# VectorE instead of GpSimd for the unit sums and three low parts in the FFN passes of a hybrid decoder step

## The chip, the cores and the metric

One Trainium2 chip, one core of it. The metric is the device time in microseconds (us) of one execution of the whole kernel. Engine names as in the profile: PE is TensorE, DVE is VectorE, ACT is ScalarE, POOL is GpSimd, SP is SyncE, which issues most DMAs.

## The reference, cut to what matters

One layer on 1024 prompt tokens and 8 sample tokens (1032 columns here), model width 1024, FFN width 2816, all in float32:

```
h = x + 0.5 * swiglu(rmsnorm(x, ffn1_norm), w_gate, w_up, w_down)
p = rmsnorm(h, mix_norm) @ w_in
h = h + concat(s5_mixer(...), short_conv(...)) @ w_out
h = h + 0.5 * swiglu(rmsnorm(h, ffn2_norm), w_gate, w_up, w_down)
y = rmsnorm(h, final_norm)
swiglu(x, wg, wu, wd) = (silu(x @ wg) * (x @ wu)) @ wd
```

The change touches only the two FFNs.

## The kernel before, in words

Activations lie transposed in SBUF, channels on partitions, the 1032 columns in three blocks of 344. Every float32 product is made of three matmuls: an operand is split into a high part (rounded to fp32r, a copy by ACT) and a low part (raw minus high, a subtraction), and PE computes high*high, high*low and low*high (`product3`, L1128 to L1130).

Both FFNs run mostly in "passes" (`ffn_passes`). A pair of passes p takes two columns of 128 of the FFN width: the even pass t computes their gate part, the odd pass t+1 their up part. The weights of a pass are four quarters of 128x512, called A11, A12, A21, A22; a Strassen-Winograd scheme needs four sums of them too: S1 = A21 + A22, S2 = S1 - A11, S3 = A11 - A21, S4 = A12 - S2. Each of the eight is a "unit" with a slot: raw `UR`, high `UH`, low `UL`. UL lies on the memory of UR, so a raw unit that is still to be read must be read before its low part is made. A21 and A22 are loaded into two staging tiles `AST`; the others into their slot.

A pass has eleven products in the order V1a, V1b, M1, M2, M6, M5, M7, V2a, M3, M4, V2b, each of four chunks, each chunk of three matmuls; chunks are numbered 0 to 43. In an even pass PE puts one step of the down projection of the pair before behind each chunk from number 7 on (36 steps, of which eight, named P1 and P2, are twice as long). DVE adds each step's bank to HT (`step_add`, L2549), which frees the bank: five banks go round, and the step that next uses a bank waits for that addition (`pair_free`).

Work around it in a pass: ACT makes the eight high parts of the next pass in an order written out by hand, copies M1, M6 and M7 out of PSUM ("copied"; M6 waits for the copy of M1, M7 for that of M6, in the same bank), and does silu. DVE makes low parts (`unit_lo` of DVE, L2510), combines sums c11, c22, c12 (L2585; V2a, M3 and the pass after next wait for them), multiplies gate and up (L2600, L2606), mixes and splits the hidden tiles for the down projection (`mix_h` L2570, `h_lo2` L2611) and the down weights (`mix_quarter` L2523 to L2528, `quarter_lows` L2532 and L2515). DVE's order is by chunk number in even passes and by product name in odd ones. POOL makes S1 to S4 of a pass (`make`, L3188 to L3198), each after the last product of the pass before that used the slot, then the low parts of A21, A22 and S4 (L3206). PE waits for each low part by `unit_ready`.

SP issues the loads in one order. The load of A21 or A22 into AST waits until the low part of the pass before is made from that tile, and until S3 or S1 of that pass is made (L936 to L941); the loads of A11 and of down weights stand behind it in the queue.

Passes 2 to 17 are in FFN 1 and 20 to 39 in FFN 2: 36 passes, 18 pairs. The first two passes of each FFN are plain (no sums); before the first pass with sums DVE has an order of its own at the top level (`mul_plain`, `x_unit_lo`, L2623, and others).

Of the kernel before, what the change touches and what calls it, by code (L numbers as in the profile page):

```python
# [332 lines left out]
def loads_count(t, unit):  # L333

    e, n = stage(t)
    return e * (PASSES[0] - 1) + max(n, 1) if unit in (A11, A12) else e * PASSES[0] + n + 1
# [23 lines left out]
def hybrid_trunk(nc, a, o):  # L360
# [11 lines left out]
    with ctx:  # L372
# [1897 lines left out]
        def _(dve):  # L2270
# [229 lines left out]
            def unit_lo(t, k):  # L2500
                if stage(t)[1] >= 2 and k == A11:
                    dve.wait_ge(s_made, made_count(t, S3))
                if stage(t)[1] >= 2 and k in (A12, S2):
                    dve.wait_ge(s_made, made_count(t, S4))
                if k == S1:
                    dve.wait_ge(s_made, made_count(t, S2))
                slot = slot_of(t, k)
                raw = AST[k - 2] if k in (A21, A22) else UR[slot]
                dve.wait_ge(u_hi, hi_count(t, k))
                dve.tensor_tensor(UL[slot][:, :], raw[:, :], f(UH[slot][:, :]), ALU.subtract).then_inc(unit_ready[slot], 1)  # L2510
# [24 lines left out]
            def quarter_lows(n):  # L2535
                if n // 4 not in LAST_PAIR:
                    sums_lo(n)
                quarter_lo(n)
# [51 lines left out]
            def c22(t):  # L2590
                combine(t, "M5", "M7", "v", (1, 2))
# [29 lines left out]
            def x_unit_lo(e, u):  # L2621
                dve.wait_ge(xu_hi, (len(XU_ORDER) + XN) * e + XU_ORDER.index(u) + 1)
                dve.tensor_tensor(xl(e, u), t_raw(e, u), f(xh(e, u)), ALU.subtract).then_inc(xu_ready[u], 1)  # L2623

            def t_step(out, x, y, op, waits=None):
                if waits is not None:
                    dve.wait_ge(t_made, waits)
                dve.tensor_tensor(out, x, y, op).then_inc(t_made, 1)

            def ffn_passes(e):  # L2630
                for t in range(FIRST[e] + 2, LAST_PASS[e] + 1):
                    p, g = divmod(t, 2)
                    more = t < LAST_PASS[e]
                    if g == 0:
                        for chunk in range(4 * len(ORDER)):
                            for n in range(STEPS):
                                if STEP_AFTER[n] + 1 == chunk:
                                    step_add(p - 1, n)
                            if chunk == 9:
                                h_lo2(p - 1, 7)  # L2640
                            if chunk == 10:
                                h_lo2(p - 1, 8)
                            if chunk == 12 and t == FIRST[e] + 2:
                                quarter_lows(4 * p - 3)
                            if chunk == 11:
                                unit_lo(t, S2)
                            if chunk == 13:
                                unit_lo(t, S1)
                            if chunk == 14:
                                mix_quarter(4 * p - 2)  # L2650
                            if chunk == 16:
                                c11(t)
                            if chunk == 18:
                                quarter_lows(4 * p - 2)
                            if chunk == 20:
                                unit_lo(t, S3)
                            if chunk == 23:
                                mix_quarter(4 * p - 1)
                            if chunk == 26:
                                quarter_lows(4 * p - 1)  # L2660
                            if chunk == 29:
                                c22(t)
                            if chunk == 33:
                                unit_lo(t + 1, A11)
                            if chunk == 32 and p not in LAST_PAIR:
                                mix_quarter(4 * p)
                            if chunk == 35:
                                unit_lo(t + 1, S1)
                            if chunk == 37:
                                c12(t)  # L2670
                            if chunk == 39:
                                unit_lo(t + 1, A12)
                            if chunk == 41 and p in LAST_PAIR:
                                quarter_lo(4 * p)
                                quarter_lo(4 * p + 1)
                    else:
                        dve.wait_ge(pair_full, step_base(p))
                        for name in ORDER:
# [6 lines left out]
                            if name == "M1":  # L2685
                                unit_lo(t, S3)
                                h_lo2(p, 0)
                            if name == "M2":
                                c11(t)
                                mul_sum(t, "C11", (0, 1))  # L2690
                                if p not in LAST_PAIR:
                                    quarter_lows(4 * p)
                            if name == "M6" and p not in LAST_PAIR:
                                quarter_lows(4 * p + 1)
                            if name == "M7":
                                c22(t)
                                mul_sum(t, "C22", (1, 2))
                                if p not in LAST_PAIR:
                                    unit_lo(t + 1, A11)
                            if p not in LAST_PAIR:  # L2700
                                if name == "M3":
                                    c12(t)
                                    mul_sum(t, "C12", (0, 2))
                                    mix_h(p, T3)
                                    mix_h(p, T1)
                                    unit_lo(t + 1, A12)
                                    h_lo2(p, 1)
                                    mix_h(p, T2)
                                    h_lo2(p, 2)
                                if name == "M4":  # L2710
                                    mul(t, "M4", "x", (1, 1))
                                    h_lo2(p, 3)
                                    mix_h(p, T4)
                                    h_lo2(p, 4)
                                    h_lo2(p, 5)
                                if name == "V2b":
                                    mul(t, "V2b", "y", (1, 0))
                                    h_lo2(p, 6)
                                continue
# [65 lines left out]
            mul_plain(0, 3)  # L2785
            mix_h(0, T2)
            mix_h(0, T3)
            unit_lo(2, A11)
            h_lo2(0, 2)
            x_unit_lo(0, T2)  # L2790
            h_lo2(0, 3)
            mix_quarter(1)
            unit_lo(2, A12)
            mul_plain(0, 4)
            mix_h(0, T4)
# [165 lines left out]
            mul_plain(1, 3)  # L2961
            mix_h(PAIR0[1], T2)
            mix_h(PAIR0[1], T3)
            unit_lo(FIRST[1] + 2, A11)
            h_lo2(PAIR0[1], 2)
            x_unit_lo(1, T2)
            h_lo2(PAIR0[1], 3)
            mix_quarter(4 * PAIR0[1] + 1)
            unit_lo(FIRST[1] + 2, A12)
            mul_plain(1, 4)  # L2970
            mix_h(PAIR0[1], T4)
# [44 lines left out]
        def _(pool):  # L3016
# [162 lines left out]
            pool.wait_ge(consts_in, 16 * 5)  # L3179
            pool.nop().then_inc(disc_p, 2)  # L3180

            def make(t, k):

                pool.wait_ge(products, slot_free(t, k))
                if k == S1:
                    pool.wait_ge(a_in[A21], 16 * loads_count(t, A21))
                    pool.wait_ge(a_in[A22], 16 * loads_count(t, A22))
                    ins = pool.tensor_tensor(UR[S1][:, :], AST[0][:, :], AST[1][:, :], ALU.add)  # L3188
                elif k == S2:
                    pool.wait_ge(a_in[A11], 16 * loads_count(t, A11))  # L3190
                    pool.wait_ge(s_made, made_count(t, S1))
                    ins = pool.tensor_tensor(UR[S2][:, :], UR[S1][:, :], UR[A11][:, :], ALU.subtract)
                elif k == S3:
                    ins = pool.tensor_tensor(UR[S3][:, :], UR[A11][:, :], AST[0][:, :], ALU.subtract)
                else:
                    pool.wait_ge(a_in[A12], 16 * loads_count(t, A12))
                    pool.wait_ge(s_made, made_count(t, S2))
                    ins = pool.tensor_tensor(UR[S4][:, :], UR[A12][:, :], UR[S2][:, :], ALU.subtract)  # L3198
                ins.then_inc(s_made, 1)

            def unit_lo(t, k):

                pool.wait_ge(u_hi, hi_count(t, k))
# [2 lines left out]
                pool.tensor_tensor(UL[slot][:, :], raw[:, :], UH[slot][:, :].bitcast(F32), ALU.subtract  # L3206
                                   ).then_inc(unit_ready[slot], 1)

            def ffn_passes(e):
                for t in range(FIRST[e] + 2, LAST_PASS[e] + 1):  # L3210
                    make(t, S1)
                    make(t, S2)
                    make(t, S3)
                    make(t, S4)
                    unit_lo(t, A21)
                    unit_lo(t, A22)
                    unit_lo(t, S4)

            ffn_passes(0)
            norm(1)  # L3220

            tab = UNITS[("tab", 2)]
# [66 lines left out]
            for k in PLAIN_HI:  # L3289
                unit_lo(FIRST[1], k)  # L3290
            norm(2)
            ffn_passes(1)

            pool.wait_ge(gf_in, 16)
            for i, n in enumerate(BY_SCALAR):
# [23 lines left out]
```

## Time and profile before

| | |
|---|---|
| median of 3 runs | 1779.7 us (1779.49 to 1780.2) |
| the profiled execution | 1779.56 us |
| its span, first to last instruction | 1777.7 us |
| busy: PE, DVE, ACT, POOL | 1761.6, 1316.3, 652.3, 644.3 us |
| granted TensorE clock, mean | 0.998 of full |

Busy time is time in which the engine executes an instruction. The span is 1.9 us shorter than the device time of the same execution. PE's matmuls overlap, so that a row shows 320 ns for one while the next starts some 157 ns later.

### The profile page before, as it was taken

What the parts mean: (1) busy time and instruction counts of PE and PEld (TensorE: products, weight loads), DVE (VectorE), ACT (ScalarE), POOL (GpSimd) and SP (SyncE); (2) the same over time, 40 slices, a digit from 0 to 9 for tenths busy, and PEclk for the clock granted to TensorE, in tenths of its full rate; (3) what the DMA queues carried; (4) which work ended last, traced back from release to release, by engine and by line L of the source; (5) the groups of instructions that cost most, each with busy time, mean ns of one, the idle gap of its engine ahead of it and who ended that gap; (6) DMA issues with size and microseconds to landing.
All of it is one profiled execution on the core that took longest, in us unless ns stands there. A gap on an engine that the chain in (4) does not pass through costs nothing.

```text
span 1777.7 us, 31737 instructions
## 1 busy us (share of the span) xinstructions
PE 1761.6 (99%) x11953; PEld 1749.4 (98%) x11953; DVE 1316.3 (74%) x2429; ACT 652.3 (37%) x1281; POOL 644.3 (36%) x669
## 2 busy tenths in 40 slices
PE   8999999999999999999999999999999999999998
PEld 7999999999999999999999999999999999999998
DVE  7658878777877876823775769977887797788766
ACT  7411333333333333533112545333333333333324
POOL 2688232332333232203995221223233332323321
PEclk9999999999999999999999999999999999999999
DMA  6132111111111111355113501111111112111112
GB/s 174 36 131 84 54 54 48 55 48 57 46 54 54 48 54 43 143 128 128 48 42 110 174 14 54 47 56 48 54 48 54 54 43 60 48 54 48 54 49 96
DMA packets 162647, 119.75 MB, mean 67 GB/s; under 512 B 10258, under 2 KB 156242, under 8 KB 161988
## 3 DMA queue, kind: packets, MB, share of 16 engines
q1 hardware_dynamic: 157012, 110.10, 20.9%
q0 software_dynamic: 864, 5.28, 0.9%
q10 hardware_dynamic: 4624, 2.36, 0.6%
q8 instruction: 99, 1.62, 0.4%
q14 instruction: 48, 0.39, 0.1%
HBM read 102.01 MB, written 15.72 MB: 66 GB/s over the span
## 4 chain that ended last, share of the span: by engine, by line
PE 96%; DVE 2%; ACT 1%; issue 0%; DVEq 0%; POOL 0%; POOLq 0%
PE bank_pair L1128 26%; PE bank_pair L1130 25%; PE bank_pair L1129 25%; PE bank_down L1128 6%; PE bank_down L1130 6%; PE bank_down L1129 6%; DVE HT L2298 1%; DVE XL L2321 1%; PE bank_pair L1542 0%; PE bank_pair L1515 0%; PE bank_pair L1638 0%; PE bank_pair L1534 0%; PE bank_pair L1236 0%; PE bank_down L1278 0%; DVE S L2315 0%
## 5 line engine op out<-in xcount | busy, mean ns | idle before, releaser
L1128 PE MATMUL bank_pair<-XHM,U_hi 128*128 128x344 f32 x720 | 230.5, 320 | 0.2 <-DVE XLM L2343 0.2
L1129 PE MATMUL bank_pair<-XLM,U_hi 128*128 128x344 f32 x720 | 229.7, 319 | 0.0
L1130 PE MATMUL bank_pair<-XHM,U_lo 128*128 128x344 f32 x720 | 229.7, 319 | 0.0
L2549 DVE SCALAR_TENSOR_TENSOR HT<-bank_pair,HT 128x344 f32<-128x344 f32 x378 | 186.2, 508 | 51.0 <-PE bank_pair L1130 50.8
L3206 POOL TENSOR_TENSOR U_lo<-AST,U_hi 128x512 fp32r<-128x512 f32 x74 | 106.0, 1435 | 266.1 <-ACT U_hi L1702 266.1
L1128 PE MATMUL bank_pair<-XH,U_hi 128*128 128x344 f32 x608 | 194.1, 319 | 0.0
L1130 PE MATMUL bank_pair<-XH,U_lo 128*128 128x344 f32 x608 | 194.1, 319 | 0.0
L1129 PE MATMUL bank_pair<-XL,U_hi 128*128 128x344 f32 x608 | 194.0, 319 | 0.0
L1128 PE MATMUL bank_pair<-XH,WH 128*128 128x344 f32 x576 | 186.7, 324 | 5.0 <-DVE XL L2321 4.9
L1130 PE MATMUL bank_pair<-XH,WL 128*128 128x344 f32 x576 | 184.2, 320 | 0.0
L1129 PE MATMUL bank_pair<-XL,WH 128*128 128x344 f32 x576 | 184.2, 320 | 0.0
L3188 POOL TENSOR_TENSOR U_raw<-AST 128x512 f32<-128x512 f32 x36 | 48.1, 1336 | 352.3 <-PE bank_pair L1130 314.9
L1702 ACT ACTIVATE U_hi<-U_raw 128x512 fp32r<-128x512 f32 x224 | 138.9, 623 | 93.6 <-DMA U_raw<-in_ffn_w_up 47.9
L2549 DVE SCALAR_TENSOR_TENSOR HT<-bank_down,HT 128x344 f32<-128x344 f32 x270 | 133.9, 506 | 21.5 <-PE bank_down L1130 20.9
L1129 PE MATMUL bank_pair<-XLX,U_hi 128*128 128x344 f32 x448 | 143.4, 320 | 0.0
L1130 PE MATMUL bank_pair<-XHX,U_lo 128*128 128x344 f32 x448 | 143.1, 320 | 0.0
L1128 PE MATMUL bank_pair<-XHX,U_hi 128*128 128x344 f32 x448 | 143.1, 319 | 0.0
L2510 DVE TENSOR_TENSOR U_lo<-U_raw,U_hi 128x512 fp32r<-128x512 f32 x186 | 138.1, 743 | 0.0
L1128 PEld LDWEIGHTS bank_pair<-XHM,U_hi 128*128 128x128 f32 x720 | 135.2, 188 | 0.6 <-DVE XLM L2343 0.5
L1129 PEld LDWEIGHTS bank_pair<-XLM,U_hi 128*128 128x128 f32 x720 | 135.2, 188 | 0.0
L1130 PEld LDWEIGHTS bank_pair<-XHM,U_lo 128*128 128x128 f32 x720 | 135.2, 188 | 0.0
L1927 ACT ACTIVATE HH<-HR 128x344 fp32r<-128x344 f32 x110 | 52.3, 489 | 197.8 <-DVE HR L2600 79.0
(398 smaller groups left out, 4922.7 us busy)
## 6 DMA issues: line engine op xcount, KB each, us to landing
DQ_raw<-in_ffn_w_down SPq DMA_DIRECT2D x52, 256.0 KB, 2.7
U_raw<-in_ffn_w_gate SPq DMA_DIRECT2D x40, 256.0 KB, 3.0
AST<-in_ffn_w_gate SPq DMA_DIRECT2D x40, 256.0 KB, 2.9
U_raw<-in_ffn_w_up SPq DMA_DIRECT2D x40, 256.0 KB, 3.3
AST<-in_ffn_w_up SPq DMA_DIRECT2D x40, 256.0 KB, 2.9
RAW<-in_w_in SPq DMA_DIRECT2D x16, 512.0 KB, 4.0
DQR<-in_ffn_w_down SPq DMA_DIRECT2D x25, 256.0 KB, 2.6
X<-in_x_prompt SPq DMA_DIRECT2D x8, 512.0 KB, 8.6
```

The lines of the kernel that those rows point to most:

```text
L1128: pe.matmul(out, wh, xh, start=first, stop=False, skip_group_check=onto)
L1129: pe.matmul(out, wh, xl, start=False, stop=False, skip_group_check=onto)
L1130: return pe.matmul(out, wl, xh, start=False, stop=last, skip_group_check=onto)
L1702: act.activation(UH[slot][:, :], src[:, :], ACT.Copy).then_inc(u_hi, 1)
L1927: act.activation(h_hi_of(p, form), h_raw_of(p, form), ACT.Copy).then_inc(h_high, 1)
L2298: ins = dve.tensor_tensor(ht, tile, ht, ALU.add)
L2321: dve.tensor_tensor(XL[:, c, cols(tb)], ring(i), f(XH[:, c, cols(tb)]), ALU.subtract).then_inc(xn_low, 1)
L2510: dve.tensor_tensor(UL[slot][:, :], raw[:, :], f(UH[slot][:, :]), ALU.subtract).then_inc(unit_ready[slot], 1)
L2549: dve.scalar_tensor_tensor(ht, STEP_BANKS[STEP_BANK[n]][:, 0:TW], 0.5, ht, ALU.mult, ALU.add).then_inc(pair_free, 1)
L3188: ins = pool.tensor_tensor(UR[S1][:, :], AST[0][:, :], AST[1][:, :], ALU.add)
L3206: pool.tensor_tensor(UL[slot][:, :], raw[:, :], UH[slot][:, :].bitcast(F32), ALU.subtract).then_inc(unit_ready[slot], 1)
```

## The change

`make` goes from POOL's program to DVE's, without a change of its waits, and so do the low parts of A21, A22 and S4 of every pass with sums. POOL's `ffn_passes` goes. In DVE's order the new instructions stand at fixed places, in even passes by chunk, in odd passes by product, and before the first such pass of each FFN among the top level's lines.

```
             def make(t, k):
-                pool.wait_ge(products, slot_free(t, k))
+                dve.wait_ge(products, slot_free(t, k))
...
-            def ffn_passes(e):            # POOL
-                for t in range(FIRST[e] + 2, LAST_PASS[e] + 1):
-                    make(t, S1)
-                    make(t, S2)
-                    make(t, S3)
-                    make(t, S4)
-                    unit_lo(t, A21)
-                    unit_lo(t, A22)
-                    unit_lo(t, S4)
...
# DVE, even pass t
+                            if chunk == 8 and t == FIRST[e] + 2:
+                                unit_lo(t, A21)
+                            if chunk == 12:
+                                unit_lo(t, A22)
+                            if chunk == 21:
+                                unit_lo(t, S4)
+                            if chunk == 25:
+                                make(t + 1, S1)
+                            if chunk == 27:
+                                make(t + 1, S2)
+                            if chunk == 30:
+                                make(t + 1, S3)
+                            if chunk == 38:
+                                make(t + 1, S4)
+                            if chunk == 40:
+                                unit_lo(t + 1, A21)
...
# DVE, odd pass t
                             if name == "M1":
                                 unit_lo(t, S3)
                                 h_lo2(p, 0)
+                                unit_lo(t, A22)
                             if name == "M2":
                                 c11(t)
                                 mul_sum(t, "C11", (0, 1))
+                                unit_lo(t, S4)
...
                             if name == "M7":
+                                if more:
+                                    make(t + 1, S1)
                                 c22(t)
                                 mul_sum(t, "C22", (1, 2))
+                                if more:
+                                    make(t + 1, S2)
+                                    make(t + 1, S3)
                                 if p not in LAST_PAIR:
                                     unit_lo(t + 1, A11)
...
                                 if name == "M3":
                                     c12(t)
                                     mul_sum(t, "C12", (0, 2))
                                     mix_h(p, T3)
                                     mix_h(p, T1)
+                                    make(t + 1, S4)
                                     unit_lo(t + 1, A12)
+                                    unit_lo(t + 1, A21)
                                     h_lo2(p, 1)
...
# DVE, before the first pass with sums of FFN 1 (FFN 2 alike, for FIRST[1] + 2)
             mul_plain(0, 3)
             mix_h(0, T2)
             mix_h(0, T3)
+            for k in (S1, S2, S3):
+                make(2, k)
             unit_lo(2, A11)
...
             mix_quarter(1)
+            make(2, S4)
             unit_lo(2, A12)
```

## Rows read from the trace of the kernel before

**Rows 1.** The page, part 1: busy time, share of the span, instructions.

```profile
PE 1761.6 (99%) x11953; PEld 1749.4 (98%) x11953; DVE 1316.3 (74%) x2429; ACT 652.3 (37%) x1281; POOL 644.3 (36%) x669
```

**Rows 2.** Waits of PE, whole span: us in total, times, longest us.

```profile
PE bank_pair L1128 <- DVE XL L2321: 4.9, 3, 3.2
...
PE bank_pair L1128 <- DVE XLM L2343: 0.2, 1, 0.2
```

**Rows 3.** Windows (us of the stretch; busy, instructions; clock, DMA share, GB/s).

```profile
215.50:697.00 481.50, 481.50 (x3062) 481.50 (x3061) 381.82 (x732) 170.32 (x341) 150.50 (x106) 1.00 0.17 51
1125.00:1717.00 592.00, 592.00 (x3764) 592.00 (x3763) 473.70 (x911) 211.85 (x424) 185.85 (x131) 1.00 0.17 52
...
1241.20:1282.80 41.60, 41.60 (x267) 41.60 (x266) 36.72 (x75) 14.24 (x29) 10.25 (x7) 1.00 0.17 52
1282.80:1303.50 20.70, 20.70 (x133) 20.70 (x133) 12.80 (x23) 8.23 (x17) 9.56 (x7) 1.00 0.18 52
```

**Rows 4.** Unit tiles: count, min/median/max ns, first and last start.

```profile
L2510 DVE TENSOR_TENSOR U_lo<-U_raw,U_hi x186: 672/681/1352, 139.7 to 1724.0; 128x512 fp32r<-128x512 f32 x186
L3206 POOL TENSOR_TENSOR U_lo<-AST,U_hi x74: 1282/1304/1674, 212.6 to 1720.1; 128x512 fp32r<-128x512 f32 x74
L3206 POOL TENSOR_TENSOR U_lo<-U_raw,U_hi x38: 1281/1562/2007, 215.1 to 1721.3; 128x512 fp32r<-128x512 f32 x38
...
L3188 POOL TENSOR_TENSOR U_raw<-AST x36: 1283/1332/2093, 184.5 to 1697.8; 128x512 f32<-128x512 f32 x36
```

**Rows 5.** Timeline of DVE, one pair: start, duration, work, idle before.

```profile
1248.26 1.39 DVE L2611 TENSOR_TENSOR XTL<-XTR,XTH 128x344 fp32r<-128x344 f32 x1
...
1261.69 1.37 DVE L2524 TENSOR_TENSOR SR<-DQ_raw 128x128 f32<-128x128 f32 x1
...
1266.35 1.79 DVE L2515 TENSOR_TENSOR DQ_lo<-DQ_raw,DQH 128x512 fp32r<-128x512 f32 x1
1268.06 1.35 DVE L2549 SCALAR_TENSOR_TENSOR HT<-bank_pair,HT 128x344 f32<-128x344 f32 x3
1269.33 0.50 DVE L2585 TENSOR_TENSOR T<-bank_pair,T 128x344 f32<-128x344 f32 x1
```

**Rows 6.** Timeline of POOL in the same pair.

```profile
1261.58 1.33 POOL L3188 TENSOR_TENSOR U_raw<-AST 128x512 f32<-128x512 f32 x1 [10.78 <-PE bank_pair L1130]
```

**Rows 7.** Timeline of DVE in the odd pass of that pair.

```profile
1287.65 0.52 DVE L2611 TENSOR_TENSOR HL<-HR,HH 128x344 fp32r<-128x344 f32 x1
...
1299.76 0.52 DVE L2585 TENSOR_TENSOR HR<-bank_pair,HR 128x344 f32<-128x344 f32 x1 [0.61 <-PE bank_pair L1130]
...
1301.50 1.49 DVE L2570 TENSOR_TENSOR XTR<-HR 128x344 f32<-128x344 f32 x1
...
1303.94 0.51 DVE L2611 TENSOR_TENSOR HL<-HR,HH 128x344 fp32r<-128x344 f32 x1
```

**Rows 8.** Timeline of ACT in the odd pass.

```profile
1291.84 0.62 ACT L1702 ACTIVATE U_hi<-U_raw 128x512 fp32r<-128x512 f32 x1
1292.36 0.44 ACT L1917 ACTIVATE HR<-bank_pair 128x344 f32<-128x344 f32 x1
```

**Rows 9.** SP's issues in the odd pass; last row: a load's landing time.

```profile
1285.56 0.37 SPq L942 DMA_DIRECT2D AST<-in_ffn_w_gate  x1
1288.45 2.25 SPq L942 DMA_DIRECT2D U_raw<-in_ffn_w_gate  x2
...
U_raw<-in_ffn_w_up SPq DMA_DIRECT2D x1, 256.0 KB, 3.2
```

**Rows 10.** Timeline of DVE before and at the first pass with sums.

```profile
201.48 0.50 DVE L2618 TENSOR_TENSOR T<-bank_pair,T 128x344 f32<-128x344 f32 x1
...
211.17 1.59 DVE L2623 TENSOR_TENSOR XLX<-XRX,XHX 128x1376 fp32r<-128x1376 f32 x1
212.83 0.52 DVE L2549 SCALAR_TENSOR_TENSOR HT<-bank_down,HT 128x344 f32<-128x344 f32 x1
213.76 0.52 DVE L2549 SCALAR_TENSOR_TENSOR HT<-bank_down,HT 128x344 f32<-128x344 f32 x1 [0.42 <-PE bank_down L1130]
```

More of the change, by code:

```diff
@@ L2623, in x_unit_lo, with make @@
                 dve.tensor_tensor(xl(e, u), t_raw(e, u), f(xh(e, u)), ALU.subtract).then_inc(xu_ready[u], 1)
+            def make(t, k):
+                dve.wait_ge(products, slot_free(t, k))
+                if k == S1:
+                    dve.wait_ge(a_in[A21], 16 * loads_count(t, A21))
+                    dve.wait_ge(a_in[A22], 16 * loads_count(t, A22))
+                    ins = dve.tensor_tensor(UR[S1][:, :], AST[0][:, :], AST[1][:, :], ALU.add)
+                elif k == S2:
+                    dve.wait_ge(a_in[A11], 16 * loads_count(t, A11))
+                    dve.wait_ge(s_made, made_count(t, S1))
+                    ins = dve.tensor_tensor(UR[S2][:, :], UR[S1][:, :], UR[A11][:, :], ALU.subtract)
+                elif k == S3:
+                    ins = dve.tensor_tensor(UR[S3][:, :], UR[A11][:, :], AST[0][:, :], ALU.subtract)
+                else:
+                    dve.wait_ge(a_in[A12], 16 * loads_count(t, A12))
+                    dve.wait_ge(s_made, made_count(t, S2))
+                    ins = dve.tensor_tensor(UR[S4][:, :], UR[A12][:, :], UR[S2][:, :], ALU.subtract)
+                ins.then_inc(s_made, 1)
             def t_step(out, x, y, op, waits=None):
@@ L2963, in _ @@
             mix_h(PAIR0[1], T3)
+            for k in (S1, S2, S3):
+                make(FIRST[1] + 2, k)
             unit_lo(FIRST[1] + 2, A11)
@@ L2968, in _ @@
             mix_quarter(4 * PAIR0[1] + 1)
+            make(FIRST[1] + 2, S4)
             unit_lo(FIRST[1] + 2, A12)
@@ L3180, in _ @@
             pool.nop().then_inc(disc_p, 2)
-            def make(t, k):
-                pool.wait_ge(products, slot_free(t, k))
[L3185 to L3199, printed above, removed]
             def unit_lo(t, k):
@@ L3207, in unit_lo @@
                                    ).then_inc(unit_ready[slot], 1)
-            def ffn_passes(e):
-                for t in range(FIRST[e] + 2, LAST_PASS[e] + 1):
-                    make(t, S1)
-                    make(t, S2)
-                    make(t, S3)
-                    make(t, S4)
-                    unit_lo(t, A21)
-                    unit_lo(t, A22)
-                    unit_lo(t, S4)
-            ffn_passes(0)
             norm(1)
@@ L3291, in _ @@
             norm(2)
-            ffn_passes(1)
             pool.wait_ge(gf_in, 16)
```

## The prediction

> **What bounds the kernel now.** I read the page's busy line first: PE is busy for 1761.6 of 1777.7 us, DVE for 1316.3, POOL for 644.3 [rows 1]. Then who PE waited for: in the whole span three waits for the low parts of the first FFN's input (4.9 us) are the largest entry, and the only one from a pass-like stage is 0.2 us at the entry of FFN 2 [rows 2]. Then the stages: from 215.5 to 697 and from 1125 to 1717 us, which is nearly all of the 36 passes, PE is busy for every one of 481.50 and 592.00 us at full granted clock [rows 3]. So in the stretches that the change touches there is nothing to win: every low part and every freed bank already comes in time. The question is only whether it still does when DVE makes them, and how much each was early.
>
> PE's clockwork gives the due times. A pair of passes is 132 groups of three matmuls (88 in the even pass with its down steps, 44 in the odd one) and takes 62.3 us (the last two windows of [rows 3] together), so a group is u = 0.472 us. The sum c12 of the odd pass starts at 1299.76, directly when M3's last group (the 36th) has ended [rows 7]; so that odd pass starts at 1299.73 - 36u = 1282.74 and its even pass at E = 1282.74 - 88u = 1241.20.
>
> **What moves.** Four `make` in each of 36 passes are 144 instructions, and of POOL's 74 + 38 low parts [rows 4] all but the four of FFN 2's first plain pass are 108: together 252, or 14 in a pair. On POOL each takes 1.3 us or more [rows 4]. On DVE a low part of the same shape takes 0.681 us (median) [rows 4]; as neighbouring DVE instructions overlap by some 0.08 us (1268.06 + 1.35 against a next start at 1269.33, [rows 5]) I count 0.60 each. DVE's price for a `make` doesn't stand in the trace: one that reads what the one before wrote can't overlap it, 0.72; 0.60 is the lower end. 14 x 0.60 = 8.4 us more DVE work in a pair, to 10.1 at the upper end.
>
> What DVE gets back: beside POOL's instructions some of DVE's are stretched. SR<-DQ_raw of 128x128, 0.28 us otherwise, took 1.37 at 1261.69, beside POOL's S1 (1261.58 to 1262.91) [rows 5, 6]; between 1241.2 and 1303.5 eight are, the first at 1248.26 (1.39), the last at 1301.50 (1.49, against 0.5) [rows 5, 7], by 7.2 us together. DVE is busy for 36.72 + 12.80 = 49.5 of 62.3 us [rows 3]; afterwards 49.5 + 8.4 - 7.2 = 50.7. Over 18 pairs: + 151 - 130, DVE ends near 1337 us of the span, POOL near 644 - 18 x 19.8 = 287.
>
> The Trainium skill ("SBUF — State Buffer", "SBUF: two separate sides") says that a port pair shared by DVE and GpSimd is an exclusive lock, which a DVE instruction with two SBUF inputs also needs, and that the loser blocks for the whole instruction. The rows agree: only two-SBUF-input instructions are stretched, the PSUM additions (0.50 to 0.52) are not. By that rule all 7.2 us come back; without it none would, which is a rival below.
>
> **Place by place in the steady pair** (before, after; due):
>
> Even pass, the tightest place: M3 waits for c22. M3's first group is number 62 of the pass, 1241.20 + 62u = 1270.46; c22 ended at 1269.33 + 0.50 = 1269.83 [rows 5], 0.63 us early, because DVE had run behind the banks. After: the down step with number n ends at E + (9 + 2n + P)u, P being the long ones so far. Step 15 ends at 1261.0, addition 0.43, mix 0.93: 1262.4. Step 16 is there at 1262.45, 17 at 1263.4; S1 until 1264.4; addition 18, two low parts of down weights until 1266.05; addition 19, S2 until 1267.1; additions 20 and 21 until 1267.95; c22 ends at 1268.45. That is 1.4 us earlier than before although two `make` stand ahead of it, since the mix (1.37 and one more) and the low part at 1266.35 (1.79) lose their stretches [rows 5]. The banks: a step bank must be added within 5u = 2.36 us (6u for M7's); the latest, number 19, is done 1.3 us after its end. From there to the pass's end the queue gets S3, S4 and the low part of A21 in chunks of 0.94 us or more that hold one addition of 0.43 and at most one 0.60: no backlog above 0.6 us. The low part of A22 and of S4 in chunks 12 and 21 come 8 us or more before M4 and M3.
>
> Odd pass, its end: the low parts of hidden tiles for the next pass's down steps. c12 at 1299.76 stays; behind it `mul_sum` and the mix T3 get back 0.6 and 1.0 (1.49 at 1301.50 [rows 7]), S4 and A21's low part cost 1.2 to 1.3. The low part that started at 1303.94 [rows 7] starts at 1303.6 and isn't due before 1303.54 + 8u = 1307.3. A12's low part ends near 1303.1, due at 1305.4.
>
> The waits that DVE now takes on itself: each `make` waits for a product. In the odd pass S1 is put before c22 and waits for M5, which ends at 1282.74 + 24u = 1294.07, while c22 can't start before M7 has ended and been copied, 1296.5. Behind S1 nothing else is queued, so nothing is lost; S2, S3 and S4 stand where their products are over. S1 also waits for A21's and A22's loads, next.
>
> Loads: SP issued A22's at 1285.56 after POOL's low part, and the next A11's at 1288.45 when its product freed it [rows 9]. After: DVE makes A22's low part behind the one at 1287.65 [rows 7], until 1288.77, so A22 is issued at 1288.8 and A11 behind it at 1289.2. Landing takes 3.2 us in such a double issue [rows 9]: 1292.4. S1 at 1294.07 isn't touched. ACT, which took A11's high part at 1291.84 and then copied M6 at 1292.36 [rows 8], does it some 0.6 us later: the copy ends at 1293.4, M7 is due at 1282.74 + 24u = 1294.07. 0.7 us are left. This is the closest place after the change. In the even pass A21's low part ends at 1280.0 instead of 1277.4 and holds up a down-weight load by 3 us: DVE's mix at the odd pass's start waits about 0.5 us, before a stretch in which it idles anyway.
>
> **Entry of each FFN** (no steady state): four `make` stand in the top-level order, and A21's low part behind the first addition. In FFN 1 DVE is free for `mul_plain(0, 3)` at 201.05 (0.4 earlier than 201.48); then four `make` with their dependences (2.9 us), less 0.6 of waits for ACT that they cover: the last x part starts at 213.15 instead of 211.17, and the first addition at 214.65 instead of 212.83 [rows 10]. Its M6 is due at: addition 1 waited for step 1 at 213.73 [rows 10], so the pass began at 208.54 and M6 at + 14u = 215.15; the addition ends at 215.17, the next, behind A21's low part, at 216.2 against 16u = 216.1. About 0.15 us lost; FFN 2's entry comes out alike. Bounds: 0, and with everything 1 us later 2 us for both. I take + 0.2.
>
> Sum: 0 for 18 pairs, + 0.2 for the entries. 1779.56 + 0.2 = 1779.8 for a run like the profiled one; that run lies 0.1 below the median, so 1779.9.
>
> **Rivals.** (a) Slower, DVE becomes the bound in the even pass: if the stretches are DVE's own and stay, c22 ends at 1269.83 + 1.2 = 1271.0, 0.6 after its due time, in each of 18 pairs: + 11, 1790.7. It decides once DVE is 0.63 us later than before at that place. For it: only the coincidence in time speaks against. The skill's "Perfetto Trace Analysis", "Optimizing Scalar/DVE Operations", would hand work of a saturated DVE to GpSimd, but adds that the two may not help each other; DVE isn't saturated here. Chance 0.03.
> (b) Slower, the load chain of the odd pass: A22's low part on DVE later than 0.7 us after my count, or landing over 3.9 us: ACT holds M6's copy, M7 waits. Another 0.5 us beyond that is 16 x 0.5 = 8 us: 1788. The three steps are regular to 0.1 us; 0.05.
> (c) Faster: PE would have to start matmuls closer together or lose waits. In the passes there is one of 0.2 us [rows 2]; 1779.5 at best from that, and over 0.2% nothing gives. 0.01.
> (d) As forecast, 0.91; its own range 1779.3 to 1781.0.
>
> 0.2% is 3.6 us, about what a measurement can tell here. Same 0.92 (the forecast and small forms of b), slower 0.07, faster 0.01. Range 1779.1 to 1782: the runs before spread over 0.7 us, and the upper side takes the entries' bound.
>
> **What would show it.** PE without waits in both long windows; DVE's low parts all near 0.68, busy near 1337; POOL without instructions in the passes, near 287; c22 of the even pass over 1 us before M3; ACT's copy of M6 within 0.7 us of before; a PE wait on HT of some tenths at each entry. Wrong: any PE wait that comes back in every pair, or stretched DVE instructions with POOL silent.

## The result, and the profile after

The changed kernel takes 1785.13 us (median of 6 runs, 1784.98 to 1786.99), the kernel before 1779.87 (6 runs, 1779.42 to 1780.59). The ratio is 1.0031 with an interval of 1.0021 to 1.0041: slower by 5.3 us, 3.7 to 7.3. Forecast were 1779.9, range 1779.1 to 1782.0, with 0.07 on slower. The forecast was wrong. Most of the loss came the way of rival (b), which had 0.05, though as single events and not in every pair; the rest came at the entries and in even passes.

Part 1 of the page, of the kernel after, answers to [rows 1]; below it the page's chain by engine. The span is 1784.3 us, 6.6 more than before. That is more than the 5.3 of the medians, as this execution (1786.19) lies 1.1 above its kernel's median and the one profiled before (1779.56) 0.3 below.

```profile
PE 1764.1 (99%) x11953; PEld 1749.5 (98%) x11953; DVE 1347.3 (76%) x2681; ACT 664.0 (37%) x1281; POOL 283.0 (16%) x417
...
PE 95%; DVE 3%; DMA 1%; ACT 1%; issue 0%; SPq 0%; DVEq 0%; POOL 0%; POOLq 0%
```

252 instructions went from POOL to DVE, DVE is busy for 1347 us (1337 was counted), POOL for 283 (287). New is that a DMA stands in the chain. DVE's new instructions, from the view of the unit tiles (count, min/median/max ns), answer to [rows 4]:

```profile
L2510 DVE TENSOR_TENSOR U_lo<-U_raw,U_hi x222: 678/682/961, 139.6 to 1734.1; 128x512 fp32r<-128x512 f32 x111
...
L2631 DVE TENSOR_TENSOR U_raw<-AST x36: 679/682/689, 202.4 to 1706.7; 128x512 f32<-128x512 f32 x36
```

A sum costs what a low part does, and in the passes nothing is stretched any more: the longest sum of its 36 is 689 ns, where low parts on DVE reached 1352 [rows 4].

The stages, as in [rows 3], and who PE waited for (us in total, times, longest), as in [rows 2]:

```profile
215.50:697.00 481.50, 478.78 (x3037) 477.73 (x3037) 394.84 (x838) 174.28 (x340) 0.00 (x0) 1.00 0.17 51
...
1125.00:1717.00 592.00, 590.74 (x3749) 589.53 (x3748) 489.55 (x1039) 220.07 (x428) 0.00 (x0) 1.00 0.17 52
```

```profile
PE bank_pair L1128 <- ACT HR L1917: 3.5, 3, 1.5
...
PE bank_down L1128 <- issue: 0.5, 2, 0.3
...
PE bank_pair L1128 <- ACT S L1917: 0.2, 1, 0.2
```

Both stretches lost their full cover. L1917 is ACT's copy of a product out of PSUM, here of M6. The view counts idle time only, and a matmul's row (320 ns) reaches over the start of the next, so it hides 0.16 us of each stop. Counted from the starts of neighbouring matmuls (their distance less 0.157, the start behind the stop included), PE's stops in the passes are:

```
kernel before: none of 0.05 or more from 205 to 700 and from 1115 to 1722 us
kernel after:  entries 214.7 0.58, 1127.1 0.61                             1.19
               odd passes, before M7: 261.8 1.28, 325.4 1.75, 1298.6 0.10,
                                      1485.9 0.23, 1548.4 1.18             4.54
               even passes, before M7: 229.9 0.18, 544.7 0.41, 1329.4 0.28 0.87
                                                                       sum 6.60
```

That is the 6.6 us of the span. The three large stops are single events in 3 of 16 odd passes, not a tax on every pass. One of them from the chain in order of time (start, us, what):

```profile
255.70 0.48 DVE HL L2611
256.17 0.61 DVE U_lo L2510
256.79 0.02 issue
256.80 0.37 SPq L942
257.17 0.04 issue
257.22 4.78 DMA U_raw<-in_ffn_w_gate
261.99 0.02 issue
262.02 0.03 ACT U_hi L1702
262.04 0.51 issue
262.55 0.45 ACT HR L1917
```

DVE makes A22's low part behind a hidden tile's; with its end SP issues A22 and then A11; A11 lands 4.78 us later; ACT, which stood at A11's high part, comes to the copy of M6 0.5 us after that; then M7 may start. Every odd pass is made of the same links. Issues of SP, then ACT, near 1294 us, where [rows 8, 9] show them in the kernel before:

```profile
1293.87 0.37 SPq L942 DMA_DIRECT2D AST<-in_ffn_w_gate  x1
1294.29 1.30 SPq L942 DMA_DIRECT2D U_raw<-in_ffn_w_gate  x2
```

```profile
1297.70 0.63 ACT L1702 ACTIVATE U_hi<-U_raw 128x512 fp32r<-128x512 f32 x1 [0.88 <-DMA U_raw<-in_ffn_w_gate]
1298.24 0.44 ACT L1917 ACTIVATE HR<-bank_pair 128x344 f32<-128x344 f32 x1
```

A11 lands 3.4 us after its issue, and the copy ends at 1298.68. M7's first matmul would have started at 1298.80 (one step of 0.157 behind the matmul before it), but it starts some 0.14 behind the end of a copy that it waits for: this pass stops for 0.1. All 16 odd passes that load for a next one, with A11's issue counted from M7's due start less 24 groups:

```
                A11 issued   landed in      copy ends, against   PE's stop
                                            M7's due start
kernel before   5.86         2.79 to 3.04   1.1 early            0
kernel after:
  261.93        6.61         4.78           1.06 late            1.28
  325.51        7.73         4.12           1.53 late            1.75
  1298.80       6.81         3.39           0.13 early           0.10
  1486.07       7.03         3.30           0.00                 0.23
  1548.60       6.63         4.67           0.96 late            1.18
  11 others     6.61 to 6.75 3.25 to 3.47   0.24 to 0.45 early   0
```

In the kernel after it is 1.00 us from landing to the copy's end in all 16. So a pass stops by issue + landing + 1.14 less 11.33 (24 groups), and 0.08 for the start behind. There are two ways to a stop: A11 lands late (261.93, 1548.60), or it is issued late (1298.80, 1486.07). The longest stop has both, and of its 1.75 us the late issue makes 1.1. The late issue comes from further back; DVE, then SP, ahead of the stop at 325.4:

```profile
317.73 0.29 DVE L2523 TENSOR_TENSOR SR<-DQ_raw 128x128 f32<-128x128 f32 x1 [3.30 <-DMA DQ_raw<-in_ffn_w_down]
...
320.78 0.68 DVE L2510 TENSOR_TENSOR U_lo<-AST,U_hi 128x512 fp32r<-128x512 f32 x1
```

```profile
312.17 0.51 SPq L954 DMA_DIRECT2D DQ_raw<-in_ffn_w_down  x1
...
321.49 0.37 SPq L942 DMA_DIRECT2D AST<-in_ffn_w_gate  x1
321.92 0.49 SPq L942 DMA_DIRECT2D U_raw<-in_ffn_w_gate  x1
```

A load of down weights, issued at 312.17, lands in 5.49 us; DVE's `mix_quarter` waits 3.30 us for it, and A22's low part stands behind that in DVE's order. The change sends this load 2.8 us later than before (2.0 us ahead of the odd pass's start instead of 4.8), as A21's low part now ends later. It lands in 3.1 to 3.8 us in 12 of the 16 passes and in 4.5 to 5.5 in four, and those four are the ones whose A11 leaves at 6.75 or later.

### The profile page after: what moved, and what is told of

Its sections match the earlier page's. It is cut to its first block, busy times and chain, and to the rows that moved or that the text cites. A ratio compares the mean times of both kernels' runs of the same rounds, so it can differ in the third digit from the quotient of the medians.

```text
span 1784.3 us, 31737 instructions
## 1 busy us (share of the span) xinstructions
PE 1764.1 (99%) x11953; PEld 1749.5 (98%) x11953; DVE 1347.3 (76%) x2681; ACT 664.0 (37%) x1281; POOL 283.0 (16%) x417
## 4 chain that ended last, share of the span: by engine, by line
PE 95%; DVE 3%; DMA 1%; ACT 1%; issue 0%; SPq 0%; DVEq 0%; POOL 0%; POOLq 0%
PE bank_pair L1128 25%; PE bank_pair L1130 25%; PE bank_pair L1129 25%; PE bank_down L1128 6%; PE bank_down L1130 5%; PE bank_down L1129 5%; DMA U_raw<-in_ffn_w_gate 1%; DVE HT L2298 1%; DVE XL L2321 1%; PE bank_pair L1542 0%; PE bank_pair L1515 0%; PE bank_pair L1638 0%; PE bank_pair L1534 0%; PE bank_pair L1236 0%; PE bank_down L1278 0%
## 5 line engine op out<-in xcount | busy, mean ns | idle before, releaser
L2549 DVE SCALAR_TENSOR_TENSOR HT<-bank_pair,HT 128x344 f32<-128x344 f32 x378 | 190.2, 512 | 58.1 <-PE bank_pair L1130 56.2
L2510 DVE TENSOR_TENSOR U_lo<-U_raw,U_hi 128x512 fp32r<-128x512 f32 x222 | 152.2, 686 | 1.2
L3316 POOL TENSOR_TENSOR OUT<-OUT,GF 128x1024 f32<-128x1024 f32 x2 | 4.7, 2374 | 697.7 <-ACT OUT L2262 697.7
L1128 PEld LDWEIGHTS bank_pair<-XH,WH 128*128 128x128 f32 x576 | 108.6, 188 | 6.3 <-DVE WL L2284 3.3
L1128 PEld LDWEIGHTS bank_pair<-XH,U_hi 128*128 128x128 f32 x608 | 114.4, 188 | 0.0
```

The lines of the kernel that those rows point to most:

```text
L1128: pe.matmul(out, wh, xh, start=first, stop=False, skip_group_check=onto)
L2549: dve.scalar_tensor_tensor(ht, STEP_BANKS[STEP_BANK[n]][:, 0:TW], 0.5, ht, ALU.mult, ALU.add).then_inc(pair_free, 1)
L3316: pool.tensor_tensor(OUT[:, n % 4, :], OUT[:, n % 4, :], GF[:, :], ALU.mult).then_inc(out_gained, 1)
```

## The experiments

Each run is compared with the kernel before, timed with it on the same chip; medians, with the ratio and its interval. The kernel after was not timed again beside them, so a version is set against it by what each loses to the kernel before: 5.3 us for the kernel after. The theory, T: in the odd pass A22's low part stands late in DVE's order, so A22 and behind it A11 are issued late; mostly that is covered, but a load that lands late isn't, because ACT's copy of M6 is queued behind A11's high part. (T as it was put on record names late landings only; the late down-weight loads above belong to it, as they too act through the place of A22's low part.) At the entries DVE's top-level order has got too long.

**One half each.** x1_lows_only gives the four sums back to POOL, x2_makes_only the three low parts.

```
x1:  -   every dve make(...) line       +   POOL: make(t, S1) ... make(t, S4) in each pass
x2:  -   every added dve unit_lo line   +   POOL: unit_lo(t, A21), (t, A22), (t, S4)
```

> The kernel after, with the four sums given back to GpSimd; VectorE keeps the three low parts. Theory T (the load of A22, and behind it in SP's queue A11, go out late in the odd pass because A22's low part stands late in VectorE's order; a load that lands late then holds ScalarE, its copy of M6 and PE's M7; plus 1.2 us at the two entries from the work put into VectorE's top-level order): the odd-pass stalls stay (about 4 us), the entries' mostly go, 1783.5 to 1784.5 us, A11's issue in the odd pass still 6.5 us after its start. Rival R (the sums on VectorE are what makes PE late, as each waits for a product and holds VectorE): 1780. Rival C (VectorE runs behind the banks once GpSimd stretches it again): 1788 or more.

> The kernel after, with the three low parts given back to GpSimd; VectorE keeps the four sums. Theory T: A22 and A11 are issued in the odd pass as in the kernel before (2.8 and 5.7 us after its start), no stall before M7 but by chance; only the entries lose up to 1 us: 1780 to 1781 us. Rival R (the sums are the cause): 1784 to 1785.

x1: 1783.49 us (9 runs), 1.0021 (1.0011 to 1.0030). x2: 1781.71 (11 runs), 1.0009 (1.0000 to 1.0018); the kernel before, 1780.26 (30 runs). PE's stops in x1 are 1.31 at 261.4, 1.45 at 1545.7, 0.34 and small ones, none at the entries; in x2 only the entries', 0.50 and 0.28 in FFN 1, 0.52 and 0.27 in FFN 2, 1.57 together. The issues of SP in the same odd pass, x1 first:

```profile
1291.19 0.37 SPq L942 DMA_DIRECT2D AST<-in_ffn_w_gate  x1
1291.61 1.26 SPq L942 DMA_DIRECT2D U_raw<-in_ffn_w_gate  x2
```

```profile
1287.19 0.37 SPq L942 DMA_DIRECT2D AST<-in_ffn_w_gate  x1
1290.09 2.25 SPq L942 DMA_DIRECT2D U_raw<-in_ffn_w_gate  x2
```

In x2 A22 is out early and A11 waits for its product, as in [rows 9]; in x1 the three loads leave within 1.3 us. So the low parts cost in the steady passes, the sums at the entries. x2's 1781.71 is 0.7 above the upper end of what was expected of it: its second stop at each entry (0.28, 0.27) is not in the kernel after. It comes while GpSimd, which has the low parts again, stretches one of DVE's (1.36 us at 218.34, 1.35 at 1127.19); that this stretch is its cause is not shown.

**One line moved.** x3_a22_early.

```
                             if name == "V1a":
+                                unit_lo(t, A22)
                                 if p not in LAST_PAIR:
                                     mix_quarter(4 * p + 1)
...
                             if name == "M1":
                                 h_lo2(p, 0)
-                                unit_lo(t, A22)
```

> The kernel after, with one line moved: in the odd pass VectorE makes A22's low part first, ahead of its down-weight sums, in a time in which it idles. Theory T: A22 is issued some 5 us earlier, A11 when its product frees it, and no M7 waits: 1785.1 less 3 to 4 = 1781 to 1782 us, the entries' 1.2 us stay. Rival R: 1785. Rival L (loads land late because of how many are in flight, wherever they are issued): 1784 to 1785.

1781.26 (11 runs), 1.0008 (0.9999 to 1.0017). All stops before M7 in odd passes are gone; the entries' 0.57 and 0.60 stay, and one of 0.62 in an even pass. DVE does the same work; only the place of 16 to 18 instructions differs, and the loss is 1.0 us instead of 5.3. In four odd passes of x3 the down-weight load still lands in 4.5 to 5.1 us, and A11 leaves at 5.86 in all 16: with A22's low part ahead of the mix, both ways to a late A11 are closed.

**The entries.** x4_entry puts S1 and S2 ahead of `mul_plain(e, 2)`, S3 and S4 ahead of `mul_plain(e, 3)`.

> The kernel after, with the four sums of the first pass with sums placed earlier in VectorE's top-level order (two ahead of mul_plain 2, two ahead of mul_plain 3, where it idles). Theory T: the waits of PE at 214.7 and 1127.1 us go, all else stays: 1785.1 less 1.2 = 1783.9 us. Rival: the entries' loss comes from A21's low part behind the first addition: under 0.3 us gained.

1784.38 (10 runs), 1.0024 (1.0015 to 1.0033): a loss of 4.1 us instead of 5.3, which alone is within the spread. The trace is clear: PE doesn't stop at either entry, and stops before M7 stay (1.19 at 260.1, 0.48 at 510.6, 0.39 at 1482.4, 1.42 at 1545.1 and two small ones). DVE's lines at the first entry, kernel after, then x4 ([rows 10] in the kernel before):

```profile
213.17 1.59 DVE L2623 TENSOR_TENSOR XLX<-XRX,XHX 128x1376 fp32r<-128x1376 f32 x1
214.67 0.51 DVE L2549 SCALAR_TENSOR_TENSOR HT<-bank_down,HT 128x344 f32<-128x344 f32 x1
```

```profile
211.30 1.58 DVE L2623 TENSOR_TENSOR XLX<-XRX,XHX 128x1376 fp32r<-128x1376 f32 x1
212.80 0.51 DVE L2549 SCALAR_TENSOR_TENSOR HT<-bank_down,HT 128x344 f32<-128x344 f32 x1
```

The same four sums cost nothing where DVE waits for a product anyway, and 1.9 us of lateness where it doesn't.

**The queue on ACT.** x5_act_order leaves the loads late and moves ACT's copy.

```
                         h_hi2(p, 1)
+                        copy_sum(t, "M6", (0, 2))
                         if more:
                             unit_hi(t + 1, A11)
-                        copy_sum(t, "M6", (0, 2))
```

(and in the even pass ahead of the high part of A12.)

> The kernel after, with only ScalarE's order changed: the copy of M6 stands ahead of the high part of A11 in the odd pass and ahead of that of A12 in the even pass. The loads stay as late as in the kernel after. Theory T (the late load costs only because the copy is queued behind it): the waits of PE before M7 go in both kinds of pass, 1785.1 less 3.2 less 0.7 = 1781.2 us; 1.2 us of the entries stay; A11 is issued 6.5 us after the odd pass's start as before the edit. Rival (the late high part itself is what PE waits for): 1785.

1781.25 (11 runs, 1780.73 to 1781.49), 1.0007 (0.9998 to 1.0015): a loss of 1.0 us. The issues are as late as in the kernel after (6.6 to 6.9), the first A11 load even lands in 4.9 us (4.8 there), and PE stops only at the entries. SP, then ACT:

```profile
1290.89 0.37 SPq L942 DMA_DIRECT2D AST<-in_ffn_w_gate  x1
1291.31 1.22 SPq L942 DMA_DIRECT2D U_raw<-in_ffn_w_gate  x2
```

```profile
1294.05 0.46 ACT L1917 ACTIVATE HR<-bank_pair 128x344 f32<-128x344 f32 x1 [0.28 <-PE bank_pair L1130]
1294.63 0.63 ACT L1702 ACTIVATE U_hi<-U_raw 128x512 fp32r<-128x512 f32 x1
```

**The lateness alone, in the kernel before.** x6_before_late, and x12_late_and_order, which adds the ACT order to it.

```
                     if FIRST[e] + 1 < t + 1 < end:
+                        if g == 1 and t > FIRST[e] + 2:
+                            sp.wait_ge(summed, sum_count(t, "C11"))
                         load_unit(t + 1, A11)
```

> The kernel BEFORE (GpSimd makes everything), with one wait added in SP's queue: in odd passes A11 is loaded only when the sum c11 is made, some 8.1 us after the pass's start instead of 5.7. VectorE and GpSimd are untouched. Theory T: A11 lands 11.3 us after the start, ScalarE copies M6 about 1 us later than PE's M7 is due, in 16 odd passes: 1780 + 16 = 1796 us (1792 to 1800), and PE's waits all before M7. Rival (the time is VectorE's added work, the loads are beside the point): 1780.

> The kernel BEFORE with the wait of x6_before_late in SP's queue (A11 of the odd pass loaded 2.4 us later) and the ScalarE order of x5_act_order (copy of M6 ahead of the high parts). Theory T (a late A11 costs only through what is queued behind it on ScalarE): all 16 waits of PE go, 1800.2 falls to 1780.2 plus at most 1 us. Rival (the late high part is itself waited for): over 1790.

x6: 1800.19 (4 runs), 1.0111 (1.0096 to 1.0127), 20 us slower with DVE and POOL doing what they did before. x12: 1780.48 (10 runs), 1.0003 (0.9994 to 1.0012). PE's waits in x6 (its lines are two further down):

```profile
PE bank_pair L1130 <- ACT HR L1919: 15.4, 16, 1.2
```

Sixteen waits in sixteen passes, a stop of 1.1 to 1.4 us each by matmul starts; the expectation counted 1.0, and the time lies at the top of its range. Three even passes stop too (0.43, 0.26 and 0.46), behind A12 loads that land in 5.1 to 5.3 us. The late load is sufficient for a loss, and the place of the copy on ACT's queue is what turns it into one.

**Why some loads land late.** A 256 KB load in the passes lands in 2.6 to 3.5 us mostly. In the kernel after (stretches 217 to 690 and 1125 to 1712 us) 22 of 204 loads take 4.0 or more (to a tenth): 15 of the 36 for which a 16 KB packet of the instruction queue q8 starts between 1.0 and 3.5 us behind the issue, and 7 of the 168 others (in x11, below, 15 of 36 and 8 of 168). In the kernel before it is 9 of 200: 4 of 23 and 5 of 177. The bounds of 1.0 and 3.5 us were not set before the traces were read. The loads around the stop at 261.8 us, from the DMA view of 256.5 to 264 us (queues with packets, MB and share; issues with KB each and median us to landing, A11 and A12 together):

```profile
q1 hardware_dynamic: 1584, 0.79, 36.8%
q8 instruction: 1, 0.02, 0.8%
issues: line engine op xcount, KB each, median us to landing
U_raw<-in_ffn_w_gate SPq DMA_DIRECT2D x2, 256.0 KB, 4.6
```

TensorE has some 25400 instructions in the trace and q8 99 packets, one for 257; that q8 carries TensorE's instructions is inferred from this. x10_fetch_phase was to shift them by 128 empty instructions on TensorE, x11_fetch_phase2 by 64 real ones.

```
x10:      keep_clock(AB[0][0], 12)  and then  for _ in range(128): pe.nop()
x11: -    keep_clock(AB[0][0], 12)      +  keep_clock(AB[0][0], 44)
```

> The kernel after with 128 empty instructions on TensorE near the start, where it waits for the input. Theory F (the loads that land over 4 us late are those that meet a 16 KB instruction load of queue q8, which comes after every 256 instructions of TensorE): the instruction loads come some 9 us earlier in the passes' frame; the waits of PE at 261.8 and 1548.4 us go, one near 325 us stays or others appear where an instruction load meets A11's; the total moves by a few us either way, 1782 to 1787. Rival (long landings are tied to the addresses loaded): the same loads land late, waits at the same places as in the kernel after, 1785.1 plus what the empty instructions take.

> The kernel after with 32 more transposes on TensorE near the start (64 instructions more on its queue; they cost a constant few us there). TensorE's trace has 25402 instructions and queue q8 99 packets of 16 KB, one for every 256. Theory F (a load lands over 4 us late when it meets such an instruction load): seen from the passes, all q8 packets come some 4.6 us earlier; the A11 loads near 257 and 1543 us of the kernel after meet none and land in 3.3 to 3.6 us, and the waits of PE at 261.8 and 1548.4 us go; waits may appear where q8 packets now meet A11's loads. Rival (late landings are tied to the addresses loaded or to the place in the program): the same A11 loads land in 4.7 us and more, the same waits of PE.

x10: 1785.30 (8 runs); the q8 packets stayed mostly within 3 us of where they were, the trace has no instruction more, and stops came at 261.2 (1.29), 1483.3 (0.55) and 1546.2 (1.30) again; the one near 325 did not. The edit didn't shift anything, so it tells nothing between the two explanations. x11: 1790.94 (5 runs), of which some 4 us is the longer start. Here the packets moved, and the stops with them: none near 261 or 1548, but 390.7 1.11, 454.2 0.71, 1177.1 1.44, 1240.8 0.66, 1678.1 1.25. At 390.7, 1177.1 and 1678.1 A11 landed late (4.6 to 4.9); at 454.2 and 1240.8 it landed in 3.5 and 3.3 but was issued 0.7 and 0.9 late, behind down-weight loads that landed in 5.1 and 5.2. The DMA view of 260.5 to 267 us, around the A11 load at 261.19, and of 385.5 to 392, around that at 386.17:

```profile
q1 hardware_dynamic: 1584, 0.79, 41.4%
issues: line engine op xcount, KB each, median us to landing
U_raw<-in_ffn_w_gate SPq DMA_DIRECT2D x2, 256.0 KB, 3.4
...
q1 hardware_dynamic: 1584, 0.79, 42.1%
q8 instruction: 1, 0.02, 0.9%
issues: line engine op xcount, KB each, median us to landing
U_raw<-in_ffn_w_gate SPq DMA_DIRECT2D x2, 256.0 KB, 4.5
```

The weights loaded at 261.19 are those that landed in 4.78 us in the kernel after and in 3.35 here. Late landings are not tied to what is loaded, and they moved when TensorE's instruction loads were moved. That a packet delays the load, and how, is not shown; there is a coincidence: it holds for 257.22, 1543.90 (kernel after), 386.17, 1172.55 and 1673.60 (x11), with q8's packet 1.8 to 2.2 us behind the issue each time, and not for every late load.

**Together.** x8_best has x3, x4 and x5; x9_before_order is the kernel before with x5's order.

> The kernel after with three edits together: A22's low part first in the odd pass, ScalarE's copy of M6 ahead of the high parts, the entry's four sums in VectorE's idle time. Theory T: no wait of PE is left in the passes, 1779.8 to 1780.3 us, level with the kernel before; as PE is busy throughout, not faster than it by more than 0.3 us. Rival (a cost of VectorE's added work remains, spread out): 1781 or more.

> The kernel BEFORE with only the ScalarE order of x5_act_order. Theory T: nothing to win, as PE waits for nothing in the passes of the kernel before: 1780.0 to 1780.3 us, within 0.1% of before. Rival (small waits of under 0.1 us are spread over the passes): 1779 or less.

x8: 1780.14 (11 runs; one of them, 4459.39, is no time of the kernel and doesn't touch the median), 0.9999 (0.9990 to 1.0008). x9: 1780.20 (11 runs), 0.9999 (0.9991 to 1.0008). In the passes of x8 PE stops only at FFN 2's entry, for 0.2 us. DVE can do all of it at no cost that these runs can tell, and nobody gains by it: no version beat the kernel before.

## Why the prediction was wrong

**Right.** The price of DVE's work and of the lost stretches: 14 instructions of 0.60 apart in a pair, 1337 against 1347 us. The even pass: c22 was counted at 26.8 us behind the pass's start and comes at 26.6, so DVE is not the bound (rival a fell). The clockwork of the odd pass, in its regular passes: A22's low part at 5.34 (measured 5.3), A22's issue at 6.1 (6.05), A11's at 6.5 (6.5), S1 ahead of c22 without loss. (These are counted from the prediction's start of the pass, which lies 0.16 behind that of the table.) Even the entry: the last x part at 213.15 and the first addition at 214.65 were counted, 213.17 and 214.67 measured.

**The step that failed** is the one on the loads: "Landing takes 3.2 us in such a double issue [rows 9]: 1292.4 ... 0.7 us are left. This is the closest place after the change." A single typical landing was set against the slack and the result booked as zero. Four things are wrong in it.

- The slack. M7 was taken as due when the group before it has ended, 1294.07; in the kernel before its first matmul starts at 1293.91, and it needs 0.14 us from the copy's end. Of 0.7 us 0.4 were there.
- The ordinary landing. A22, A11 and A12 now leave within 1.3 us, and A11 lands in 3.25 to 3.47 us also when nothing disturbs it. In ordinary passes 0.1 to 0.3 us are left.
- The tail of the landing. In 3 of 16 odd passes it took 4.1 to 4.8 us. The kernel before has a tail too (4.8 at most in its passes, for other loads), behind a slack that allowed 4.3 us for A11; the change cut this to 3.6.
- The issue. The prediction saw that A21's later low part holds up a down-weight load by 3 us (2.8 measured) and let DVE's mix wait "about 0.5 us, before a stretch in which it idles anyway". The mix waits 1.0 to 1.7 us in ordinary passes and up to 3.4 in four, and in those four this outlasts the idle stretch and delays A22's low part, A22 and A11 by 0.1 to 1.1 us.

Rival (b) named the mechanism, place and chain, and both of its conditions, a low part late by over 0.7 us and a landing over 3.9, came true in single passes; it got 0.05 because "the three steps are regular to 0.1 us". In the kernel before they are (A11 leaves at 5.86 in all 16 passes), in the kernel after neither the issue nor the landing is. x5 and x12 show the missing half, that the price comes from ACT's order and not from A11 being needed.

**The entries** were mis-sized: + 0.2 was taken, 1.19 measured, inside the bound of 2. DVE's times were right; PE's weren't. The matmul that uses the bank was taken as due at 215.15; the kernel before starts it at 214.98, and the kernel after would have at 214.86. A stop also costs a restart: the addition ends at 215.18, the matmul starts 0.10 us later, and the next start and one more together lose another 0.16. So near misses became 0.58.

**The 0.87 us of even passes** has another place: A12 is issued there 6.0 us before M7 is due, in both kernels, and a landing over some 4.9 us stops PE; in the three passes that stop it took 5.0 to 5.2. The kernel before has the same weak place: its longest A12 landing in the profile, 4.69, was covered by 0.2 us, and in x6, with VectorE and GpSimd as before, three landings of 5.1 to 5.3 did stop PE. x9 finds no time in it (1780.20 against 1780.15). Whether the change makes long landings more frequent (22 of 204 against 9 of 200 loads) or the two profiles differ by chance stays open.

By the sum: entries 1.19, odd passes 4.54, even 0.87 make the profiled 6.6; in the medians x3 or x5 leaves 1.0 of the 5.3, x8 nothing.

## What to carry to other kernels

A slack against a DMA is measured against the tail of its landing times, not their median: list every landing in the stage, and where the slack is below the longest one count the events and their price. The loads further back in the chain count as well: here a late down-weight load acted through two engines' queues on another load. The slack itself ends where the matmul would have started, less what it needs behind its releaser, not where the group before it ends. When work is moved to an engine that is not the bound, follow what its end releases in the load queue, and what stands behind the waiting instruction on the engine that takes the load; here one move of a copy (x5), or of one low part (x3), was worth nearly the whole steady loss. New work belongs where the engine's row shows idle time before the next instruction (x4), not where it is first needed.

## What the runs showed of the hardware

With GpSimd silent, VectorE's 128x512 subtractions took 682 ns in the median and 689 at most for the sums, where up to 1352 ns had occurred beside GpSimd [rows 4]. This agrees with the lock that the Trainium skill describes ("SBUF — State Buffer", "SBUF: two separate sides"). The stretches in the passes of the kernel before come to some 127 us (130 were counted); in the kernel after there is none. Packets of 16 KB arrive on q8, some 18 us apart in the passes (99 for some 25400 TensorE instructions), and a 256 KB load with the start of such a packet 1.0 to 3.5 us behind its issue took 4.0 us or more in 15 of 36 cases, against 7 of 168 (kernel before: 4 of 23 and 5 of 177). 64 more instructions at the start moved which loads these were. A matmul that had to wait for a copy or an addition (the stops before M7 and at 214.7 and 1127.1) started 0.10 to 0.15 us behind its end, and the next start was 0.235 us away instead of 0.157.
